# Loading order at the start of a two-layer float32 kernel: which queue brings the first x tile, the columns and the Fourier table, and in what pieces the table's low part is taken

## The reference, cut to what matters

```python
sh1, sc1, gt1, sh2, sc2, gt2 = silu(c) @ w_mod + b_mod      # six vectors of 1024
a = rms_norm(x, g_norm_mix) * (1 + sc1) + sh1
f = fft2(a in 4 groups of 256 features, axes=(tokens, features)).real
h = x + gt1 * (f @ w_fnet_out)
```

## Time and profile before

| | |
|---|---|
| median of three runs | 1567.5 us |
| the profiled execution, its own time | 1566.53 us |
| its span, first to last instruction | 1564.7 us |
| mean granted TensorE clock | 0.997 |
| TensorE busy | 1545.1 us, 99% |
| VectorE, ScalarE, GpSimd busy | 768.3, 309.2, 1002.3 us |
| read from HBM | 169.86 MB |

### The profile page before, as it was taken

One profiled execution on the slowest core, in us unless ns is written; L12 is line 12 of the kernel. 1 busy time (PEld: TensorE's weight loads), 2 busy tenths in 40 slices (PEclk: granted clock), 3 DMA queues, 4 the chain that ended last, 5 costly groups with the idle time before them and its releaser, 6 DMA issues.

```text
span 1564.7 us, 19571 instructions
## 1 busy us (share of the span) xinstructions
PE 1545.1 (99%) x7096; PEld 1287.1 (82%) x7096; DVE 768.3 (49%) x876; ACT 309.2 (20%) x477; POOL 1002.3 (64%) x792
## 2 busy tenths in 40 slices
PE   7999999999999999999999999999999999999997
PEld 6998888887887888888888888888888888888886
DVE  7875555564427565244154665456576434343013
ACT  6542111110111001112032122212322111111001
POOL 4736666667666666766556576475567667676664
PEclk9999999999999999999999999999999999999999
DMA  9962333322333333332323232232233333332331
GB/s 369 404 239 81 99 102 94 94 94 94 94 108 95 94 94 101 112 94 81 106 68 95 68 95 88 82 95 80 67 94 95 94 99 100 96 94 94 97 104 56
DMA packets 218119, 172.52 MB, mean 110 GB/s; under 512 B 5216, under 2 KB 191968, under 8 KB 218080
## 3 DMA queue, kind: packets, MB, share of 16 engines
q1 hardware_dynamic: 218080, 171.98, 34.9%
HBM read 169.86 MB, written 2.10 MB: 110 GB/s over the span
## 4 chain that ended last, share of the span: by engine, by line
PE 95%; DVE 1%; DMA 1%; SPq 1%; POOL 1%; issue 0%; ACT 0%; POOLq 0%; DVEq 0%
PE ps L571 32%; PE ps L575 31%; PE ps L574 31%; DMA mod_early<-in_w_mod_t 1%; POOL w_lo L549 0%; DVE act_lo L1393 0%; SPq L313 0%; POOL w_hi L547 0%; SPq L321 0%; PE ps L654 0%; PE ps L898 0%; DVE mod_early L1304 0%; SPq L333 0%; PE ps L753 0%; DVE res L1509 0%
## 5 line engine op out<-in xcount | busy, mean ns | idle before, releaser
L549 POOL TENSOR_TENSOR w_lo<-raw,w_hi 128x1024 fp32r<-128x1024 f32 x248 | 622.2, 2509 | 20.7
L571 PE MATMUL ps<-act_hi,w_hi 128*128 128x512 f32 (+1 forms) x1304 | 506.1, 388 | 0.2 <-DVE act_lo L1393 0.2
L575 PE MATMUL ps<-act_lo,w_hi 128*128 128x512 f32 (+1 forms) x1304 | 503.1, 386 | 0.0
L574 PE MATMUL ps<-act_hi,w_lo 128*128 128x512 f32 (+1 forms) x1304 | 502.9, 386 | 0.0
L546 POOL TENSOR_TENSOR w_hi<-raw,zero 128x1 fp32r<-128x1 f32 x248 | 55.9, 225 | 489.2 <-PE ps L571 489.2
L571 PEld LDWEIGHTS ps<-act_hi,w_hi 128*128 128x128 f32 x1304 | 245.7, 188 | 51.4 <-issue 1.7
L574 PEld LDWEIGHTS ps<-act_hi,w_lo 128*128 128x128 f32 x1304 | 245.7, 188 | 49.7 <-issue 1.4
L575 PEld LDWEIGHTS ps<-act_lo,w_hi 128*128 128x128 f32 x1304 | 245.6, 188 | 49.4
L547 POOL TENSOR_SCALAR w_hi<-raw 128x1023 fp32r<-128x1023 f32 x248 | 269.5, 1087 | 0.0
L571 PE MATMUL ps<-wide_hi,w_hi 128*128 128x512 f32 (+2 forms) x624 | 240.2, 385 | 2.2 <-POOL w_lo L549 1.7
L574 PE MATMUL ps<-wide_hi,w_lo 128*128 128x512 f32 (+2 forms) x624 | 239.5, 384 | 0.0
(11 more groups left out here) (193 smaller groups left out, 1445.2 us busy)
## 6 DMA issues: line engine op xcount, KB each, us to landing
raw<-in_w_in SPq DMA_DIRECT2D x88, 512.0 KB, 4.0
gates<-in_w_mod_t SPq DMA_DIRECT2D x20, 1024.0 KB, 11.3
raw<-in_w_ffn_up SPq DMA_DIRECT2D x40, 512.0 KB, 3.9
raw<-in_w_ffn_down SPq DMA_DIRECT2D x22, 512.0 KB, 3.8
raw<-in_w_ff_gate SPq DMA_DIRECT2D x22, 512.0 KB, 3.9
raw<-in_w_ff_up SPq DMA_DIRECT2D x22, 512.0 KB, 4.0
raw<-in_w_ff_down SPq DMA_DIRECT2D x22, 512.0 KB, 3.8
raw<-in_w_r_out SPq DMA_DIRECT2D x16, 512.0 KB, 3.5
```

The source lines that it names most:

```text
L549: nc.gpsimd.tensor_tensor(w_lo[:, two, :], raw[:, slot, :], f32(w_hi[:, two, :]), SUB).then_inc(split_done, 1)
L571: ins = mm(o, w, a, start=start, stop=False)
L574: mm(o, wl, a, start=False, stop=False)
L575: return mm(o, w, al, start=False, stop=stop)
```

## The change

x tiles 0 to 3 become SP's first four transfers. ScalarE issues four transfers itself, ahead of its wait for `early_loaded`: the columns, table half 0, the identity, table half 1, in this order. The identity goes to free columns of `tmp[:, 4]` beside the small vectors, where it was in `tmp[:, 0]`. The low part of the table is taken by four subtractions of 128 by 512, one for each row tile, where it was two of 128 by 1024; VectorE does them in a new order, TensorE waits for row tile k alone, and the counts of `dft_split` in the waits of SP and TensorE are adapted. The high parts stay two instructions of GpSimd.

```diff
-        identity = tmp[:, 0, 0:P]
+        identity = early[:, EARLY + 80:EARLY + 80 + P]
...
-            sp.dma_start(early[:, 0:EARLY], t["columns"][:, 0:EARLY]).then_inc(early_loaded, 16)
-            sp.dma_start(identity, t["identity"]).then_inc(early_loaded, 16)
-            x_tile(0)
-            dft_table(0)
-            x_tile(1)
-            dft_table(1)
-            x_tile(2)
-            x_tile(3)
+            for a in range(TT):
+                x_tile(a)
             mod_chunk(1, [0, 1])
...
-            sp.wait_ge(dft_split, 1)
+            sp.wait_ge(dft_split, 2)
             fnet_panel(1)
-            sp.wait_ge(dft_split, 2)
+            sp.wait_ge(dft_split, 4)
             fnet_panel(2)
...
-            sp.wait_ge(dft_split, 3)
+            sp.wait_ge(dft_split, TT + 1)
...
-                        pe.wait_ge(dft_split, k // 2 + 1)
+                        pe.wait_ge(dft_split, k + 1)
...
-            pe.wait_ge(dft_split, 3)
+            pe.wait_ge(dft_split, TT + 1)
...
+            act.dma_start(early[:, 0:EARLY], t["columns"][:, 0:EARLY]).then_inc(early_loaded, 16)
+            dft_view = t["dft_tokens"].rearrange("(k p) n -> p k n", k=TT)
+            for n in range(2):
+                act.dma_start(raw[:, n, :].rearrange("p (k n) -> p k n", k=2), dft_view[:, 2 * n:2 * n + 2, :]).then_inc(dft_loaded[n], 16)
+                if n == 0:
+                    act.dma_start(identity, t["identity"]).then_inc(early_loaded, 16)
             act.wait_ge(early_loaded, 32)
...
-            def dft_lo(n):
-                dve.wait_ge(dft_hi_made, n + 1)
-                hi, lo = (flat(w, S_DFT + 2 * n) for w in (wide_hi, wide_lo))
-                tt(lo, raw[:, n, :], f32(hi), SUB).then_inc(dft_split, 1)
+            def dft_lo(k):
+                dve.wait_ge(dft_hi_made, k // 2 + 1)
+                hi, lo = (w[:, S_DFT + k, :] for w in (wide_hi, wide_lo))
+                tt(lo, raw[:, k // 2, k % 2 * T:(k % 2 + 1) * T], f32(hi), SUB).then_inc(dft_split, 1)
...
             x_rstds(0)
             dft_lo(0)
             x_lo(0)
+            dft_lo(1)
             x_rstds(1)
-            dft_lo(1)
+            dft_lo(2)
             x_rstds(2)
             x_lo(1)
+            dft_lo(3)
             x_rstds(3)
```

More of the change, by code:

```diff
@@ L326, in fnet_panel @@
                 sp.dma_start(raw[:, slot, :], t["w_fnet_panels"][m]).then_inc(raw_loaded[slot], 16)
-            def dft_table(n):
-                sp.dma_start(raw[:, n, :].rearrange("p (k n) -> p k n", k=2), view(t["dft_tokens"], TT)[:, 2 * n:2 * n + 2, :]
-                             ).then_inc(dft_loaded[n], 16)
             def x_tile(a):
                 sp.dma_start(x_tok[:, a, :], t["x"][a * P:(a + 1) * P, :]).then_inc(x_loaded[a], 16)
-            sp.dma_start(early[:, 0:EARLY], t["columns"][:, 0:EARLY]).then_inc(early_loaded, 16)
-            sp.dma_start(identity, t["identity"]).then_inc(early_loaded, 16)
-            x_tile(0)
-            dft_table(0)
-            x_tile(1)
-            dft_table(1)
-            x_tile(2)
-            x_tile(3)
+            for a in range(TT):
+                x_tile(a)
             mod_chunk(1, [0, 1])
```

## The result

The changed kernel takes 1576.87 us, the median of six runs (1574.99 to 1578.11), against 1566.47 for the kernel before in the same comparison: a ratio of 1.0063, 95% interval 1.0053 to 1.0073. It is slower by 10.4 us, where +2.0 was forecast, outside the range.

A forecast was written before the change was run, and what follows sets the result against it. TensorE was taken as the bound, its early work set by ScalarE, VectorE and the w_mod transfer. Identity delay +3.62, less 1.14 and 0.52 us of idling, gave +2.0 on 1567.5: 1569.5 us, range 1566.2 to 1571.5.

The forecast's parts named there:

- waiting silu: ScalarE's silu at the start waits for the identity until about 7.5 us; its first wait ended at 3.07 before.
- closing of ScalarE's 1.14 us: ScalarE's 1.14 us of idling before squaring x tile 2 disappears, leaving +2.5 us for its later work.
- VectorE's 0.52 us: VectorE's 0.52 us of idling for the w_mod transfer to `mod_early` closes and covers that much of the delay.
- covered split: VectorE's four table subtractions, 2.7 us for 2.4, are hidden; without cover the fourth costs at most 0.67 us.
- nearly unchanged rest behind the third mark: Later work, here from the first 512-column output matmul: from 38 us everything follows TensorE, nothing gives the delay back.
- SP's head start: SP issues x tile 0 0.92 us earlier; its whole stream, w_mod included, gains about 0.7 us.
- The identity behind the table: On ScalarE's queue the identity lands with table half 0 at best, at 7.5 us, between 6.8 and 8.3.
- E: Time at which the identity has landed and ScalarE's first wait ends, taken as 7.5 us.
- rival C: SP's queue is served first, all x tiles ahead of the identity: landing 10.3, net +4.8, 1572.3 us; chance 0.10.
- The sum's rule: Net change of the whole time is the identity's landing time minus 5.5 us, giving +2.0 us.
- the level therefore costs nothing: TensorE's clock level at the first transforms costs nothing: even at first slow, it reaches row tile 2 at 21.1.

The follow-up runs named there:

- e7: The kernel before with only the table's low part taken per row tile, its order and its waits: 1566.74 us, ratio 0.9999.
- e5: The kernel before with the issues of columns and identity moved from SP to ScalarE, SP issuing all the rest: 1570.92 us, ratio 1.0025.
- e6: The changed kernel with columns and identity back at the head of SP's queue, ScalarE issuing only the two table halves: 1571.22 us, ratio 1.0027.
- e10: The changed kernel with each x tile loaded as two transfers of 2 KB rows: 1574.02 us, ratio 1.0039.
- e11: The changed kernel with the identity in two transfers of 256 B rows: 1578.07 us, ratio 1.0064.
- e1: The changed kernel with ScalarE issuing the identity before table half 0: 1573.08 us, ratio 1.0043.
- e9: The changed kernel with columns and identity joined in one transfer of 800 B rows, first on ScalarE's queue: 1569.43 us, ratio 1.0014.
- e3: The changed kernel with GpSimd's four products on mod_early held until VectorE has made the first two u low parts: 1570.92 us, ratio 1.0029.
- e13: The kernel before with GpSimd computing the feature table's low part three times: 1570.72 us, ratio 1.0019.
- e4: The changed kernel with the second feature product repeated three times, 18 more matmuls ahead of the third feature tile: 1575.33 us, ratio 1.0061.

## Why the prediction was wrong

**What held.** The waiting silu, the closing of ScalarE's 1.14 us and of VectorE's 0.52 us, the covered split (e7) and the nearly unchanged rest behind the third mark came out as written. SP's head start did too: in e5, where GpSimd's products waited for their transfer, they started at 25.85, against 26.81 before. So did the first order of causes: a wait for the identity takes the place of what was removed.

**The step that failed first** is "The identity behind the table": E was set at 7.5, with 6.8 and 8.3 as bounds, and was 10.52. The turns were counted for the table's rows against x's, at one byte to two. The columns (rows of 288 B) and the identity (512 B) were left at that byte ratio, though each of their pieces costs a whole 4 KB piece of x as well. Counted in pieces it is 8 + 16 + 8 = 32 on ScalarE's side, against 32 of 4 KB, all four x tiles: 2048 + 612 = 2660 KB, and 11.26 − 0.92 = 10.3. That number stood in rival C, under another mechanism. "SP's queue is served first" is refuted by e6, where ScalarE's table landed first, and by e10 and e11, which move E to 7.32 and 12.05 by the size of pieces alone. That C's number came out is luck.

The count by pieces also gives the other landings of the changed kernel: table half 0 at 8.9 (GpSimd took it up at 9.17) and half 1 at 14.1 (14.49). E comes out within 0.5 us in e1, e9, e10, e11 and the changed kernel. It is no general rule: e6's half 1 landed 2.5 us ahead of it, and in e5, where 868 KB should pass by it, the silu started at 6.22, later than at 6.12 in e1 with 1124 KB. How the engines share when both queues hold short rows stays open. The Trainium skill (DMA: Bandwidth & Descriptors, "Queues, rings and completion order") has each engine take turns between queues at packet granularity. The taking of turns agrees. The prediction read it as speaking for near-equal bytes, which does not follow when one queue's rows are 288 B to 2 KB and the other's 4 KB. A turn of 9 to 17 descriptors does not fit either: by my estimate from the page's figure, each of ScalarE's four transfers would then be one turn, half 1 would pass beside four x tiles at most and land by 11.6 us, and it was taken up at 14.49.

**The sum's rule**, net = E − 5.5, would have given +5.0 with the right E. The third tile moved by 6.6. Of this 2.15 us are VectorE's pair, 3.57 instead of 1.42, and 4.5 the rest, 0.5 less than the rule; e3, without the meeting, has the third tile 4.5 us late. With the 2.0 us of half clock this makes up the +8.5 us: 4.5 where 2.0 was forecast, and two terms that the sum put at nothing. With the right E alone the forecast would have been 1572.5, and still too low.

**The second miss** is that pair. Following ScalarE's delay up to 33 us, I shifted VectorE's work as a block and looked at its waits alone, not at who runs beside it. GpSimd's products started at about 27 us in both kernels, before by their own transfer (26.81), after right behind GpSimd's low part of the feature table (27.25); VectorE's pair moved from 24.5 into them. e3 and e13 show the cost from both sides. Low parts whose input is in PSUM kept their 1.40 us a pair beside the same products. The Trainium skill (SBUF — State Buffer, "Who interferes with whom") states this: a VectorE instruction with two SBUF inputs contends with a GpSimd instruction that reads SBUF, while one with at most one SBUF input, outside the two-port modes, does not. The rows agree, and the rule would have named the pair beforehand.

**The third miss**: "the level therefore costs nothing" was argued for the start only. The longer gap before the third tile, 2.65 us for 1.10, was followed by half clock, which cost 2.0 us; e3 and e4 shorten the gap, one by holding GpSimd back, one by work added, and the clock stays up.

**What stays open.** The median lies 1.9 us above the profiled execution. Its untraced runs have a mean clock of 0.994 to 0.995, for 0.994 in the traced one, so the record does not explain these 1.9 us. In e9, whose runs spread over 9 us, the three at 1566 us have a clock of 0.996 and the three above 1573 have 0.993 to 0.994, so there the length of the dips is a likely cause, but only one execution of each kernel is traced. What sets the length of the second dip (9.3, 10.8 or 12.4 us in its column) is open too.

## What to carry to other kernels

A small transfer that an engine needs early must stand ahead of large ones in every queue, its own and the others: when two queues share the DMA engines, bytes alone do not give the landing, since short rows lose against long ones; join small transfers into one with longer rows (4.82 us for 6.12 here). When a chain is delayed, ask not only who waits for it but whom it now runs beside. A delay that opens a long enough gap on TensorE is paid twice, once as the gap and once in the clock.

## What the runs showed of the hardware that was not expected

- Beside x in rows of 4 KB, two queues shared the engines by pieces: 754 to 710 packets in 12 us at 2.83 to 0.93 MB. 100 KB took until 6.1 us as two transfers (e1), and until 4.8 as one (e9). With short rows in both queues this did not hold: 457 to 290 packets in 5 us (e6).
- Two VectorE low parts with both inputs in SBUF took 3.6 to 5.8 us beside GpSimd's products of two SBUF inputs, and 1.42 alone; a pair with one input in PSUM took 1.40 beside them.
- After an idle 2.65 us TensorE ran at granted clock 0.50 for 6 us, though it had been busy for 25 us ahead of that; with 0.5 to 1.65 us of idling in the same place the matmuls behind it kept their pace.
- The stretch from the one-column matmuls on took 9.3, 10.8 or 12.4 us in the traces, with or without a dip ahead of it (e4: 12.42 without, e13: 12.40 with).
- Being ahead at 58 us did not help in e7: 1.3 us won by then met a wait of 1.2 us at 93.
